# The per-layer gate projection as seven block products per pair of tiles, in a one-layer hybrid decoder trunk

## What is computed

```python
h = h + f.astype(h.dtype)                                   # FFN, its second matrix is w_down
gate = jax.nn.sigmoid(rmsnorm(h, norm_ple_w[i]) @ w_pg[i])  # 2048 x 2048
h = h + ((p[i] @ w_ple[i]) * gate).astype(h.dtype)          # p: 512 x 256
return rmsnorm(h, final_norm_w)
```

## Time and profile before

| | |
|---|---|
| median of 3 runs | 2188.47 us (2188.01 to 2188.64) |
| profiled execution | 2188.78 us, span 2187.1 us |
| granted clock of PE, mean | 0.998 of full speed |
| instructions | 28802 |
| last PLE matmul starts | 1991.2 us |
| final norm begins on DVE | 2170.6 us |

### The profile page before, as it was taken

The page is one execution under the profiler, slowest core; times in us unless marked ns, Lnnn a source line. Parts: engine busy times, 40 slices in busy tenths (PEclk is TensorE's granted clock), DMA queues, the critical chain, the costliest instruction groups (busy, mean ns, idle before and its releaser), DMA issues.

```text
span 2187.1 us, 28802 instructions
## 1 busy us (share of the span) xinstructions
PE 2168.5 (99%) x10794; PEld 1834.3 (84%) x10794; DVE 1380.7 (63%) x1726; ACT 885.3 (40%) x1026; POOL 304.9 (14%) x329
## 2 busy tenths in 40 slices
PE   9999999999999999999999999999999999999997
PEld 7888878888888888888888888888888888888886
DVE  7486336453378988888888888886333333446444
ACT  6222246442243544445554454444222122226444
POOL 6993004000000111111111111110000000000001
PEclk9999999999999999999999999999999999999999
DMA  6422222134332877777777777766343332233222
GB/s 222 135 75 94 104 97 82 58 121 168 120 118 104 214 209 212 206 197 189 209 210 204 205 189 201 212 198 246 99 142 107 122 128 93 92 115 114 96 96 77
DMA packets 106181, 321.53 MB, mean 147 GB/s; under 512 B 8240, under 2 KB 57264, under 8 KB 85904
## 3 DMA queue, kind: packets, MB, share of 16 engines
q1 hardware_dynamic: 76400, 268.39, 34.3%
q0 software_dynamic: 29728, 52.44, 13.1%
HBM read 298.77 MB, written 22.02 MB: 147 GB/s over the span
## 4 chain that ended last, share of the span: by engine, by line
PE 89%; POOL 7%; ACT 1%; DVE 1%; DMA 1%; issue 0%; SPq 0%; POOLq 0%; DVEq 0%; ACTq 0%
PE bank L1016 23%; PE bank L686 17%; PE bank L687 17%; PE bank L688 17%; PE bank L1018 12%; PE bank L800 1%; DMA Y<-in_x 1%; ACT xs_hi L1126 0%; POOL QKV L2312 0%; POOL QKV L2332 0%; POOL Q L2353 0%; POOL Y L2348 0%; POOL Q L2358 0%; PE bank L870 0%; POOL QKV L2327 0%
## 5 line engine op out<-in xcount | busy, mean ns | idle before, releaser
L1016 PE MATMUL bank<-x_block,w_hi 128*128 128x512 f32 x2240 | 777.4, 391 | 1.2 <-DVE w_lo L1961 1.2
L1018 PE MATMUL bank<-x_block,w_lo 128*128 128x256 f32 x2240 | 629.0, 281 | 0.0
L1102 ACT ACTIVATE w_hi<-w_raw 128x2048 fp32r<-128x2048 f32 (+1 forms) x134 | 222.4, 1660 | 733.6 <-PE bank L688 720.9
L1016 PEld LDWEIGHTS bank<-x_block,w_hi 128*128 128x128 f32 x2240 | 419.6, 187 | 92.6 <-DVE w_lo L1961 1.5
L1018 PEld LDWEIGHTS bank<-x_block,w_lo 128*128 128x128 f32 x2240 | 423.3, 189 | 0.0
L686 PE MATMUL bank<-xs_hi,w_hi 128*128 128x512 f32 x1024 | 404.8, 395 | 2.7 <-DVE xs_lo L1578 2.2
L688 PE MATMUL bank<-xs_hi,w_lo 128*128 128x512 f32 x1024 | 398.8, 389 | 0.0
L687 PE MATMUL bank<-xs_lo,w_hi 128*128 128x512 f32 x1024 | 398.7, 389 | 0.0
L1554 DVE TENSOR_TENSOR w_lo<-w_raw,w_hi 128x2048 fp32r<-128x2048 f32 (+1 forms) x136 | 271.6, 1997 | 134.0 <-ACT w_hi L1102 131.4
L1403 ACT ACTIVATE w_hi<-Y 128x1024 fp32r<-128x1024 f32 x159 | 168.7, 1062 | 180.0 <-PE bank L1018 125.2
L686 PEld LDWEIGHTS bank<-xs_hi,w_hi 128*128 128x128 f32 x1024 | 192.2, 188 | 46.9 <-issue 5.6
(11 more groups left out here) (356 smaller groups left out, 2505.5 us busy)
## 6 DMA issues: line engine op xcount, KB each, us to landing
w_raw<-in_w_up SPq DMA_DIRECT2D x48, 1024.0 KB, 5.1
w_raw<-in_w_down SPq DMA_DIRECT2D x64, 704.0 KB, 4.1
Y<-in_w_up SPq DMA_DIRECT2D x40, 1024.0 KB, 6.0
w_raw<-in_w_in SPq DMA_DIRECT2D x31, 1024.0 KB, 4.9
Y<-in_w_up POOLq DMA_DIRECT2D x59, 512.0 KB, 6.8
Y<-in_w_up SPq DMA_DIRECT2D x39, 512.0 KB, 7.6
w_raw<-in_w_out SPq DMA_DIRECT2D x16, 1024.0 KB, 5.3
w_raw<-in_w_pg SPq DMA_DIRECT2D x16, 1024.0 KB, 4.7
```

The lines of the kernel that those rows point to most:

```text
L1016: nc.tensor.matmul(place(c, b, 0, 2), w_h[:, ks], xb[b][:, k, :, :].rearrange("p e t -> p (e t)"), start=fresh and k == 0, stop=False, ski ...
L1018: last = nc.tensor.matmul(place(c, b), w_l[:, ks], xb[b][:, k, 0, :], start=False, stop=k == HALF_K - 1, skip_group_check=True)
L1102: nc.scalar.activation(w_hi[c % 2][:, 0:width], w_raw[c % 2][:, 0:width], ACT.Copy).then_inc(hi_made, 1)
```

## The change

The gate projection takes the block form, two output tiles ("gate" row 2c and "value" row 2c+1, both of the same projection) a pair, eight pairs.

- The seven activation blocks `gb` are made while the last down quarter runs. Its tiles are computed in the order of rows 0, 8, 1, 9, ... (`last_row`; w_down is laid out so). SP parks each finished row in DRAM, ACT scales it by the norm gain in place and makes halves, DVE makes the sums of blocks and the rests, 256 columns at a time. Three blocks (A12, A22, S4) are made whole, 2048 columns at a time, during and after the PLE tiles.
- PLE tiles use seven banks in turn (0 for tile 15, after tile 12). ACT copies them to six staging slots, SP writes each to DRAM; a row comes back when it is needed.
- Each product is three matmuls of 256 columns into one place. All four sums of weight blocks are made by DVE. 1/rms is spread by PE behind the second product of pair 0.
- Squares go to `h_ss` by accumulating DMAs of POOL's queue; rows of h come back from DRAM two at a time.
- Tail: eight short matmuls for `h_ss` and eight for the last value row's square, then as before. The last gate row is finished in two halves.
- The gate loops are written out, no longer hardware loops.

The core of the diff (SP, PE, ACT, DVE, POOL in this order; declarations, semaphore aliases and helpers that the text describes are left out):

```diff
+            def gate_raw_in(c, b):
+
+                if c == 0:
+                    sp.wait_ge(lo_made, PLE0 + (1 if b in (S3, A22) else 2))
+                elif b == A11:
+                    sp.wait_ge(blk_lo, gate_index(c - 1, S1) + 1)
+                elif b == S3:
+                    sp.wait_ge(g_sums, G_SUMS + 4 * c)
+                else:
+                    sp.wait_ge(blk_lo, gate_index(c - 1, b) + 1)
+                part = slice(BLOCK, 2 * BLOCK) if b in (A12, A22) else slice(0, BLOCK)
+                sp.dma_start(gate_raw(c, b), A["w_pg"][2 * c + (b in (S3, A22))][:, part]).then_inc(raw_in[b], 16)
+
...
+            for b in (S3, A22, A11, A12):
+                gate_raw_in(0, b)
+            for j in range(KT):
+                sp.wait_ge(ple_out, j + 1)
+                sp.dma_start(ple_dram[:, j, :], ple_stage[:, j % PLE_SLOTS, :]).then_inc(ple_sent[j % PLE_SLOTS][0], 16)
+            ple_all_sent(sp)
...
+            for c in range(GATES):
+                if c:
+                    ple_row_in(2 * c - 1)
+                if c < GATES - 1:
+                    gate_raw_in(c + 1, S3)
+                    gate_raw_in(c + 1, A11)
+                    gate_raw_in(c + 1, A12)
+                if c:
+                    ple_row_in(2 * c)
+                    h_rows_in(c)
+                if c < GATES - 1:
+                    gate_raw_in(c + 1, A22)
...
                 for u in range(PLE_PER):
                     j = PLE_PER * s + u
-                    if j >= 4:
-                        pe.wait_ge(ple_out, j - 3)
+                    if PLE_BANKS[j] in PLE_BANKS[:j]:
+                        pe.wait_ge(ple_out, j - PLE_BANKS[:j][::-1].index(PLE_BANKS[j]))
+                    elif PLE_BANKS[j] < 2:
+                        pe.wait_ge(evacuated, DOWN_END)
...
+                if s == 0:
+                    sum_tokens(3 * KT, [h_ss], bank[2], sum_spread)
...
+                for b in range(PRODUCTS):
+                    pe.wait_ge(blk_lo, gate_index(c, b) + 1)
+                    if c == 0:
+                        pe.wait_ge(gb_lo, GB_LO + 4 * HALF_K + (LATE.index(b) + 1 if b in LATE else 0))
+                        if b == 0:
+                            pe.wait_ge(ple_out, KT - 2)
+                    if c == 1 and b == 0:
+                        pe.wait_ge(evacuated, DOWN_END)
+                        pe.wait_ge(ple_out, KT)
+                        pe.wait_ge(rstd_made, 3)
+                    if c >= 2 and b == 0:
+                        pe.wait_ge(c12_made, FAST + c - 1)
+                    if b == A12:
+                        pe.wait_ge(u2_made, FAST + c + 1)
+                    if b == A22:
+                        pe.wait_ge(u3_made, FAST + c + 1)
+                    if b == S4:
+                        pe.wait_ge(c22_made, FAST + c + 1)
+                    fresh = b in (S3, S2, A11, S1)
+                    w_h, w_l = ring(w_hi, FAST + c, b), ring(w_lo, FAST + c, b)
+                    for k in range(HALF_K):
+                        ks = slice(k * P, (k + 1) * P)
+                        last = product(place(FAST + c, b), w_h[:, ks], w_l[:, ks], gb[b][:, k, 0, :], gb[b][:, k, 1, :],
+                                       fresh and k == 0, k == HALF_K - 1, onto=True)
+                    last.then_inc(product_done, 1)
+                    if c == 0 and b == S3:
+                        spread(diag_made, 3, c_value, bank[2], rstd_spread)
+
...
+            def ple_copy(j):
+
+                if j >= PLE_SLOTS:
+                    ple_row_sent(act, j - PLE_SLOTS)
+                act.wait_ge(ple_done, j + 1)
+                nc.scalar.activation(ple_stage[:, j % PLE_SLOTS, :], bank[PLE_BANKS[j]][:], ACT.Copy).then_inc(ple_out, 1)
+
+            def late_half(b, src):
+
+                act.wait_ge(h_scaled, H_SCALED + KT)
+                if b == A22:
+                    act.wait_ge(t_made, T_MADE + 4 * HALF_K)
+                if b == S4:
+                    ple_all_sent(act)
+                nc.scalar.activation(gb[b][:, :, 0, :], src, ACT.Copy).then_inc(gb_hi, 1)
+
+            def gate_half(c, b):
+
+                if b in (A11, A12, A22):
+                    act.wait_ge(raw_in[b], RAW_IN + 16 * (c + 1))
+                if b in (S3, S2, S1, S4):
+                    act.wait_ge(g_sums, G_SUMS + 4 * c + {S3: 1, S2: 2, S1: 3, S4: 4}[b])
+                if c == 0 and b < RING:
+                    act.wait_ge(ple_done, KT if b >= 2 else PLE_PER)
+                else:
+                    act.wait_ge(product_done, gate_index(c, b) - (RING - 1))
+                nc.scalar.activation(ring(w_hi, FAST + c, b), gate_raw(c, b), ACT.Copy).then_inc(blk_hi, 1)
...
+            ple_copy(0)
+            second_sum_half(6)
+            scale_h(7)
+            ple_copy(1)
+            w_half(PLE0 + 1)
+            ple_copy(2)
+            first_sums_half(7)
+            for j in range(3, 6):
+                ple_copy(j)
+            second_sum_half(7)
+            for j in range(6, 8):
+                ple_copy(j)
+            late_half(A12, B21)
+            for j in range(8, 10):
+                ple_copy(j)
+            gate_half(0, A11)
+            ple_copy(10)
+            gate_half(0, S3)
+            for j in range(11, KT):
+                ple_copy(j)
+            gate_half(0, S2)
+            gate_half(0, S1)
+            late_half(A22, T4)
+            root(2, norm4[:, 1, :], norm4[:, 0, :])
+            late_half(S4, B22)
...
+            for c in range(GATES):
+                if c:
+                    gate_half(c, S1)
+                gate_half(c, A12)
+                if c:
+                    gate_square(c, c_value, 2 * c - 1, value_h, value_sq)
+                    gate_sigmoid(c, c_gate, gate_ready, gate_made)
+                gate_half(c, A22)
+                if c:
+                    gate_square(c, c_gate, 2 * c - 2, h_made, gate_sq)
+                if c == 0:
+                    act.wait_ge(rstd_spread, 3)
+                    nc.scalar.activation(rstd[:], bank[2][:], ACT.Copy).then_inc(rstd_made, 1)
+                gate_half(c, S4)
...
+            first_rests(6)
+            second_rest(6)
+            first_sums(7)
+            w_rest(PLE0 + 1)
+            first_rests(7)
+            second_rest(7)
...
+            late_rest(A12, B21)
+            gate_s3(0)
+            gate_rest(0, A11)
+            gate_rest(0, S3)
+            gate_sums(0)
+            gate_rest(0, S2)
+            gate_rest(0, S1)
+            late_rest(A22, T4)
+            dve.wait_ge(ple_done, KT)
+            dve.wait_ge(sum_spread, 3)
+            rms_small(bank[2], 1.0 / D, var_made, root_made, diag_made, 3, c_value)
+            gate_rest(0, A12)
+            late_rest(S4, B22)
+            dve.wait_ge(gb_lo, GB_LO + PRODUCTS * HALF_K - 3 * (HALF_K - 1))
+            gate_s4(0)
+
...
+            for c in range(GATES):
+                if c:
+                    gate_c12(c - 1)
+                    gate_rest(c, S1)
+                if c:
+                    gate_rest(c, A12)
+                    finish_gate(c - 1)
+                gate_rest(c, A22)
+                gate_u(c)
+                if c == 0:
+                    dve.wait_ge(rstd_made, 3)
+                gate_rest(c, S4)
+                gate_c22(c)
+                if c < GATES - 1:
+                    gate_rest(c + 1, A11)
+                    gate_s3(c + 1)
+                    gate_rest(c + 1, S3)
+                    gate_sums(c + 1)
+                gate_c11(c)
+                gate_c21(c)
+                if c < GATES - 1:
+                    gate_rest(c + 1, S2)
+                    gate_s4(c + 1)
...
+                finish_value(c)
+            gate_c12(GATES - 1)
+            finish_last(1)
...
+            def add_squares(n, done, c_tile):
+
+                pool.wait_ge(done, HEADS + n // 2 + 1)
+                if n:
+                    pool.wait_ge(ss_added, SS_ADDED + 16 * n)
+                if n == 0:
+                    pool.dma_start(h_ss[:], c_tile).then_inc(ss_added, 16)
+                else:
+                    pool.dma_start(h_ss[:], c_tile, accum_op=ALU.add).then_inc(ss_added, 16)
+
+            for c in range(GATES - 1):
+                add_squares(2 * c, value_sq, c_value)
+                add_squares(2 * c + 1, gate_sq, c_gate)
```

425 lines of the change are left out of this document (297 added, 128 removed).

## The result

The changed kernel takes 2210.35 us (median of 4 runs, 2209.26 to 2214.12); the kernel before took 2188.55 beside it. The ratio is 1.0103, with a 95% interval of 1.0085 to 1.0120. The forecast was 2194 with a range up to 2203: the sign was right, the size was not. The profiled execution took 2209.53 us (span 2208.0).

The account below looks back on a forecast made before the run. PE bounds the kernel before, DVE the steady pairs after. Gate start 27.1, gate stage 172.1 and tail 6.7 sum to 205.9 us for 200.86, plus 5.0 on 2188.8; forecast 2194 us, range 2184.5 to 2203.

Parts of the forecast that it names:

- PE's stream: Gate stage: 1344 matmuls of 256 columns at 0.120 us take 161.3 us instead of 174.1, minus 12.8.
- Rival 3: Gate matmuls: weight loads don't hide behind 256 columns, slot 0.130, 2202 us; chance 0.09, shared with slow accumulations.
- DVE becomes the bound: Steady pairs 2 to 7: DVE needs 20.7 us a pair against PE's 20.16, plus 3.2 in six.
- up to there they cost nothing: Accumulating transfers of squares: free up to 4.5 us each; at 6.8 the last two cost 2.4 more.
- transfers against each other: Transfers disturbing one another: left out of the sum without a price, named only as leaning upward.
- DVE over 95% busy: Sign to look for: DVE busy over 95% of the time from 2020 to 2160 us.
- The start: Start of the gate stage: gate begins at 27.1 us for 22.6; with the new waits plus 12.4.
- Rival 1: Start: copies keep up with PE and the norm is ready by S3; 2182 to 2184 us, chance 0.09 in full, 0.18 half.
- Rival 2: PE's gaps before tile 15 and the spread: granted clock falls once, 2196 to 2197 us; chance 0.12 (to 2199).
- Pair 0: First gate pair: 25.3 us, with PE waiting 3.2 before the spread, 0.45 for it and 1.5 before A12.
- A11 lands 46.6: Pair 1: its blocks are asked for at 41.9 us, A11 lands at 46.6; waits of 0.9 and 1.5 follow.
- The tail: Last product to final norm: 6.7 us instead of 4.1, plus 2.6.

Follow-up runs that it names:

- g1: Changed kernel without the 14 accumulating transfers of squares and with DVE's sum S3 ahead of the rest of A11 (result incomplete): 2199.2 us, ratio 1.0043.
- h1: Changed kernel with reordered SP issues, S3 before A11's rest, PLE rows sent first, ACT halves later, A11 of pair 1 asked early, shorter tail: 2187.3 us, ratio 0.9994.
- m1: k1 with the raw block S3/S2 of pair 1 in a place of its own, asked for before sum S4 of pair 0: 2184.7 us, ratio 0.9982.
- e2: Changed kernel without the 14 accumulating transfers of squares (result incomplete): 2206.0 us, ratio 1.0078.
- untouched loops: Six profiles, the changed kernel's among them, that have its steady loop unaltered: pairs 2 to 7 take 21.82 to 22.32 us each, mean 22.02.
- g2: Changed kernel with SP asking for A22 before the rows, h rows later, and DVE's sum S3 ahead of the rest of A11: 2200.8 us, ratio 1.0051.
- g3: Changed kernel with the 14 squares added by POOL instead of by accumulating transfers: 2211.5 us, ratio 1.0109.
- g4: Changed kernel with PLE rows 0 to 5 sent to DRAM before gate blocks A11 and A12 of pair 0 are asked for: 2202.1 us, ratio 1.0062.
- h4: Changed kernel with short filler matmuls in PE's two gaps, 20 ahead of the last PLE tile and 12 ahead of the spread: 2209.3 us, ratio 1.0094.
- k2: Changed kernel with the first norm's chain moved forward on ACT and DVE, u2 of pair 0 earlier, spread behind S2: 2211.5 us, ratio 1.0105.
- m2: h1 with the raw block S3/S2 of pair 1 in a place of its own: 2185.7 us, ratio 0.9985.
- e1: Changed kernel with SP asking for A22 before the PLE row and h rows, and for h rows only after sum S1: 2209.3 us, ratio 1.0096.
- k1: h1 and k2 together, with DVE's rest of A11 ahead of sum S3 again in pair 1 alone: 2186.8 us, ratio 0.9993.
- i1: Changed kernel with the 14 transfers of squares overwriting instead of adding (result incomplete): 2205.3 us, ratio 1.0074.
- e3: Changed kernel with DVE's sum S3 ahead of the rest of A11: 2210.4 us, ratio 1.0101.
- e4: Changed kernel with 36 short filler matmuls ahead of the last PLE tile and 18 ahead of the spread: 2212.2 us, ratio 1.0103.

## Why the prediction was wrong

- **PE's stream** (slot 0.120, a product 2.88, a pair 20.16): right; g1, h1 and m1 run whole pairs at 20.16. Rival 3 is out.
- **Pairs 2 to 7, the step that failed.** "DVE becomes the bound" at 20.7 was right about DVE: 20.85 without the transfers of squares, and the 1.2 hand-over is 1.12. What failed is that I let every transfer of the steady pairs pass as hidden, the squares by "up to there they cost nothing" and the raw blocks by "transfers against each other", left out of the sum with no price. I took 4.5 us for an adding transfer; they took 4.4 and 8.0; but the price isn't their own lateness. They and 3 MB more are released together, and A22 and A11 come late: 22.32 for 20.7 a pair, 9.8 in six, of which 1.5 a pair go with the squares' transfers (e2; 1.2 from the mean of the untouched loops). That arrival and not DVE's work is the cause is shown by e2, g1, g2 and g3 (whose idling is that of e2); g2 and g3 leave nothing out. The mean load, 166 GB/s, gives no sign of it: no transfer moves in a third of each pair. The sign "DVE over 95% busy" didn't follow from the sum either, in which 2.4 of the 20.7 are DVE's waits: e2, at 20.85, shows 88%.
- **The start**, 27.1 for 31.1. The chain was right (SP's order, row 0, copy 6, tile 15; g4 cuts it and 6.9 us go); two terms were mis-sized. Row 0 landed at 19.3 for 17.1 (SP's issues stand at 12.5 as forecast; the landing behind them took 6.8 for 4.6), which with ACT's queue behind it made the last PLE tile 2.6 later (28.4 for 25.8). And this tile, at the lower clock, took 2.7 for 1.36. "Rival 1", the front holding, was wrong, but its point of decision was the right place to act. The heading's "plus 12.4" is a slip: its parts, and the sum, have 4.5 + 7.6 = 12.1.
- **Rival 2, the clock**, did happen, twice, beside the forecast and not instead of it. It cost 1.4 to 1.6 at the gate's start (h4) and at most 0.4 in pair 0.
- **Pair 0**, 25.3 forecast, 25.95 measured. Where the clock stays up the parts are right as well: in g4 PE stands 3.2 ahead of the spread, which takes 0.56, and 1.2 ahead of A12, for 3.2, 0.45 and 1.5. In the changed kernel the lower clock made A11 1.1 and S2 1.7 longer, and the waits shrank by nearly as much (2.2 ahead of the spread, none ahead of A12). What the prediction did not see is that these gaps cover another chain, from sum S4 to A11 of pair 1, so that taking them out by itself gains nothing (k2).
- **Pair 1**, 22.6 for 25.3: "A11 lands 46.6" assumed 4.7 us for a block with four asked for together; ACT had it 7.5 us after the first of the four issues (2015.20 to 2022.74). The same error as in pairs 2 to 7, and these 2.8 us are the 2.7 of difference. In h1, with A11 asked for early, the pair takes 20.9, but pair 0 takes 27.9 there, and both together 48.8 for 48.4 in g2; so h1 doesn't show what the early A11 is worth by itself.
- **The tail**, 6.7 for 6.56: right, with its parts (1.31 of waiting, 1.8 of sums, 2.3 of fillers). What it left out is that the clock may fall there, 1.6 to 3.4 us up to the norm in eight of 13 profiles.

## What to carry to other kernels

When an engine that had slack is loaded until it is the bound, the transfers that its steps release arrive in bursts: cost each block from its own issue, with everything issued in the same few microseconds beside it, and not from the mean load. Put on a queue first what is waited for first, and what nobody waits for into the stretch where the transfers stand still. And before a gap of an engine is charged to the time, ask which list of the other engines it covers: here 4 us of PE's standing, with the spread behind it, cost one, while a wait for a buffer and 1 MB of loads ahead of a 256 KB row on one queue cost seven.

## What the runs showed of the hardware that I had not expected

- An adding transfer of 256 KB within SBUF takes 4.4 us for the first and 8.0 for the second square of a pair, with more transfers beside it; the same without adding 3.3 and 6.5.
- POOL's addition of 512 elements stretches DVE's two-input steps beside it by 1.1 us in all, and takes 2.28 us for 1.47 (g3).
- The granted clock fell to 0.50 at or behind the gap of PE of 4.9 to 5.4 us ahead of the last PLE tile in all 11 profiles that have it, and behind 4 us ahead of the spread (h1, m2). Shorter gaps don't decide it: it fell behind some of 1.7 to 2.0 us in pair 1 (e1, e2, g3, g4, k1) and not behind others of 2.0 (h4, i1), nor behind 2.8 to 3.1 ahead of the spread (e1, e3, g4). In eight of 13 profiles it fell behind only 1.3 us followed by 16 matmuls of one column, and in none of the five in which short matmuls follow each eight of these. Where the two gaps of the start were filled with short matmuls it stayed at 1.00 (e4, h4).
